# Modulation vectors of a ten-phase transformer kernel: the accumulator folded by DMAs instead of summed by four matmuls

## The reference, cut to what matters

```python
c_act = jax.nn.silu(c)
for layer in range(DEPTH):
    mod = c_act @ ada_w[layer] + ada_b[layer]
    sh1, sc1, g1, sh2, sc2, g2 = [m[:, None, :] for m in jnp.split(mod, 6, axis=-1)]
    hmix = rmsnorm(x, norm_mix[layer]) * (1.0 + sc1) + sh1
    ...
    x = x + g1 * y
```

## Time and profile before

| what | value |
|---|---|
| median of three runs | 1736.61 us (1735.37 to 1739.26) |
| span of the profiled execution | 1734.1 us |
| PE busy | 1708.0 us (98%) |
| DVE busy | 1412.9 us (81%) |
| POOL busy | 435.0 us, of which 267.3 us issue tiles of ada (448 DMAs) |
| DMA | 411.45 MB, mean 237 GB/s |
| PE L2535, the sums in misc | 216 rows, mean 241 ns |
| DVE L2927, multiply-adds of 128 x 512 | 420 rows, mean 751 ns |

### The profile page before, as it was taken

How to read it: one execution, slowest core, us unless ns; L and a number is a source line. 1 busy time by engine, 2 the same in 40 slices (tenths; PEclk the granted TensorE clock), 3 DMA queues, 4 the chain that set the end, 5 groups by cost and what they waited for, 6 DMA issues and landing times. The chain is left out here.

```text
span 1734.1 us, 36503 instructions
## 1 busy us (share of the span) xinstructions
PE 1708.0 (98%) x14039; PEld 1667.7 (96%) x14039; DVE 1412.9 (81%) x1924; ACT 908.4 (52%) x1274; POOL 435.0 (25%) x685
## 2 busy tenths in 40 slices
PE   7999999999999999999999999999999999999998
PEld 5999999999999999999999999999999998799998
DVE  6877898788778977898987799779988896788655
ACT  3443367764335533365634356667444567764444
POOL 6322321012223122321232224540322232401000
PEclk9999999999999999999999999999999999999999
DMA  9998858549887787867698865334988772257550
GB/s 338 356 359 279 294 178 280 166 158 321 304 304 242 276 302 270 302 212 272 229 314 305 302 199 191 115 132 156 322 297 293 230 199 83 78 199 251 184 176 25
DMA packets 261793, 411.45 MB, mean 237 GB/s; under 512 B 21950, under 2 KB 204414, under 8 KB 261560
## 3 DMA queue, kind: packets, MB, share of 16 engines
q1 hardware_dynamic: 224968, 290.67, 51.0%
q0 software_dynamic: 36720, 119.36, 19.4%
HBM read 408.90 MB, written 2.63 MB: 237 GB/s over the span
## 5 line engine op out<-in xcount | busy, mean ns | idle before, releaser
L2891 DVE TENSOR_TENSOR lo<-raw,hi 128x2048 fp32r<-128x2048 f32 (+2 forms) x251 | 565.6, 2256 | 162.4 <-ACT hi L2719 161.8
L2719 ACT CAST hi<-raw 128x2048 fp32r<-128x2048 f32 (+2 forms) x266 | 497.4, 1872 | 377.6 <-PE dacc L2388 189.4
L2386 PE MATMUL up<-operand_hi,hi 128*128 128x256 f32 x1952 | 553.1, 283 | 1.4 <-DVE lo L2891 1.4
L2387 PE MATMUL up<-operand_lo,hi 128*128 128x256 f32 x1952 | 552.3, 283 | 0.0
L2388 PE MATMUL up<-operand_hi,lo 128*128 128x256 f32 x1952 | 552.3, 283 | 0.0
L2163 POOL DMA_DIRECT2D ada<-in_ada_w_dram x448 | 267.3, 613 | 841.8 <-DVE ada_acc L2927 793.5
L2386 PEld LDWEIGHTS up<-operand_hi,hi 128*128 128x128 f32 x1952 | 374.4, 192 | 2.3 <-DVE lo L2891 2.0
L2388 PEld LDWEIGHTS up<-operand_hi,lo 128*128 128x128 f32 x1952 | 374.5, 192 | 0.0
L2387 PEld LDWEIGHTS up<-operand_lo,hi 128*128 128x128 f32 x1952 | 374.5, 192 | 0.0
L2927 DVE SCALAR_TENSOR_TENSOR ada_acc<-ada,c_col,ada_acc 128x512 f32<-128x512 f32 x420 | 315.3, 751 | 13.8 <-DMA ada<-in_ada_w_dram 0.6
L2386 PE MATMUL dacc<-act_hi,hi 128*128 128x256 f32 x976 | 276.2, 283 | 0.7 <-DVE act_lo L3103 0.7
(11 more groups left out here) (483 smaller groups left out, 2858.2 us busy)
## 6 DMA issues: line engine op xcount, KB each, us to landing
ada<-in_ada_w_dram POOLq DMA_DIRECT2D x448, 256.0 KB, 4.8
raw<-in_ffn_wg_dram SPq DMA_DIRECT2D x88, 512.0 KB, 5.4
raw<-in_ffn_wu_dram SPq DMA_DIRECT2D x88, 512.0 KB, 5.2
raw<-in_ffn_wd_dram SPq DMA_DIRECT2D x88, 512.0 KB, 5.6
raw<-in_ffn_w_up_dram SPq DMA_DIRECT2D x88, 512.0 KB, 4.6
raw<-in_ffn_w_down_dram SPq DMA_DIRECT2D x46, 512.0 KB, 4.6
raw<-in_hg_w_in_dram SPq DMA_DIRECT2D x32, 512.0 KB, 4.8
raw<-in_attn_w_qkv_dram SPq DMA_DIRECT2D x24, 512.0 KB, 7.7
```

The lines of the kernel that those rows point to most:

```text
L2386: pe.matmul(o, stat[0], mov[0], start=start, stop=False, skip_group_check=True)
L2387: pe.matmul(o, stat[0], mov[1], start=False, stop=False, skip_group_check=True)
L2719: last = act.copy(put(slab(hi, s, SPL)), take(slab(raw, s, RAW)))
L2891: last = dve.tensor_tensor(put(slab(lo, s, SPL)), take(slab(raw, s, RAW)), put(slab(hi, s, SPL)).bitcast(F32), ALU.subtract)
```

## The change

Only vectors 2 to 29 are changed.

- A tile is loaded by one DMA, 128 rows on 128 partitions with all 1024 columns, and multiplied and added by one DVE instruction of 128 x 1024.
- When a vector's eight tiles are in `ada_acc` (now 128 x 1024), POOL folds it with three accumulating DMAs, each behind the landing of the one before: partitions 64 to 127 onto 0 to 63, 32 to 63 onto 0 to 31, 16 to 31 onto 0 to 15. A fourth DMA writes the 16 rows to DRAM in pieces of 128 columns, and a fifth reads them back as `folded`, 128 x 128, in which partition 16 a + r holds piece a of row r. The five count on the semaphore `folds`.
- PE sums with one matmul: `folded` against `block_ones`, 128 x 8.
- The first tile of the next vector waits on DVE for all five DMAs of the vector before (`folds`), in place of `ada_summed`.
- In the loop of a five-vector phase POOL's instructions are written out: loads 0 to 3 of the next vector, the fold of this one, loads 4 to 7. PE's sum moves from behind the ups of i = 3 to behind those of i = 4, `mod_vector` with it.
- The last vector of such a phase, and that of G, is folded by POOL in the next phase, around `pre_add`, and summed in the middle of that phase: in feed-forward phases behind the ups of block 2, in the mixers at a place of their own. In A the first tile of vector 7 also waits for the fold of vector 6.
- At the start two more small DMAs bring `c` in another layout, and the transpose of `c` has 48 rows instead of 32.

The diff, cut to its core:

```diff
@@ ada_load @@
             source = ada_source(v, k) if source is None else source
+            if v >= 2:
+                eng.dma_start(ada_place(m), source).then_inc(full, 16)
+                return
...
@@ start, SP @@
                 sp.dma_start(c_rows[r0:r0 + ASTEPS, 0:AQ],
-                             T[name].rearrange("b (i q) -> (b i) q", q=AQ)).then_inc(S["c_in"], 16)
+                             T[name].rearrange("b (i q) -> (b i) q", q=AQ)).then_inc(S["lam_in"], 16)
+                sp.dma_start(c_wide[2 * ASTEPS + r0 // AG:2 * ASTEPS + r0 // AG + KB, :],
+                             T[name].rearrange("b (k p) -> (b k) p", p=P)).then_inc(S["lam_in"], 16)
...
@@ POOL @@
+            def fold_start(v):
+                pool.wait_ge(S["ada_step"], tile_steps(tile_index(v, KB - 1) + 1))
+                if v > 2:
+                    pool.wait_ge(S["folds"], 16 * FOLDS * (v - 2))
+                pool.dma_start(ada_acc[0:64, :], ada_acc[64:128, :], accum_op=ALU.add).then_inc(S["folds"], 16)
+            def fold_rest(v):
+                n = v - 2
+                done = 16 * FOLDS * n
+                pool.wait_ge(S["folds"], done + 16)
+                pool.dma_start(ada_acc[0:32, :], ada_acc[32:64, :], accum_op=ALU.add).then_inc(S["folds"], 16)
+                pool.wait_ge(S["folds"], done + 32)
+                pool.dma_start(ada_acc[0:16, :], ada_acc[16:32, :], accum_op=ALU.add).then_inc(S["folds"], 16)
+                pool.wait_ge(S["folds"], done + 48)
+                pool.dma_start(fold_dram.rearrange("(a r) j -> r a j", a=KB),
+                               ada_acc[0:16, :].rearrange("r (a j) -> r a j", a=KB)).then_inc(S["folds"], 16)
+                pool.wait_ge(S["folds"], done + 64)
+                pool.wait_ge(S["ada_summed"], v)
+                pool.dma_start(folded[:, :], fold_dram).then_inc(S["folds"], 16)
...
+                    if left_vector(p) is not None:
+                        fold_start(left_vector(p))
                     pre_add(p)
+                    if left_vector(p) is not None:
+                        fold_rest(left_vector(p))
...
-                        with pool.Fori(0, (FI - 3) // 2) as it:
+                        for u in range(v, v + 4):
                             for k in range(KB):
-                                ada_load(pool, v + 1, k, it, w[u // n][k * P:(k + 1) * P, bass.ds(it * D + (u % n) * D, D)])
+                                if k == ATILES:
+                                    fold_start(u)
+                                    fold_rest(u)
+                                ada_load(pool, u + 1, k)
@@ ada_sum, PE @@
-                pe.wait_ge(S["ada_step"], tile_steps(tile_index(v, KB - 1) + 1) + ASTEPS * it)
                 if v >= 2:
+                    pe.wait_ge(S["folds"], 16 * FOLDS * (v - 1) + 16 * FOLDS * it)
                     pe.wait_ge(S["mod_done"], v + it)
+                    pe.matmul(o[:, 0:KB], folded[:, :], block_ones[:, :], start=True, stop=True,
+                              skip_group_check=True).then_inc(S["ada_summed"], 1)
+                    return
...
@@ ffn, PE @@
                 ups(2)
+                if left_vector(p) is not None:
+                    ada_sum(left_vector(p))
                 down(1)
...
-                        if p in five_vectors and i == 3:
+                        if p in five_vectors and i == 4:
                             ada_sum(v, it)
...
-                if p in five_vectors:
-                    ada_sum(v + 4)
@@ ada_tile, DVE @@
+                if v >= 2:
+                    c = c_col[:, 2 * ASTEPS + (KB if v >= V2 else 0) + k:2 * ASTEPS + (KB if v >= V2 else 0) + k + 1]
+                    if k == 0:
+                        dve.wait_ge(S["ada_summed"], 2)
+                        dve.wait_ge(S["folds"], 16 * FOLDS * (v - 2) + 16 * FOLDS * it)
+                        dve.tensor_scalar(ada_acc[:, :], ada_place(m), c, None, ALU.mult).then_inc(S["ada_step"], 1)
+                        return
+                    dve.wait_ge(S["ada_step"], tile_steps(m) + KB * it)
+                    dve.scalar_tensor_tensor(ada_acc[:, :], ada_place(m), c, ada_acc[:, :],
+                                             ALU.mult, ALU.add).then_inc(S["ada_step"], 1)
+                    return
```

More of the change, by code:

```diff
@@ L52 @@
 ASTEPS = KB * AG
+C_ROWS = 2 * ASTEPS + 2 * KB
+FOLDS = 5
 PE_TILES = KB // 2
@@ L124, in build @@
         ada_acc = sb("ada_acc", D)
+        folded = sb("folded", P)
         operand_hi = sb("operand_hi", KB * SEQ, F32R)
@@ L611, in pe_attention @@
             columns(2)
-            columns(3, lambda: square_sums(0))
+            columns(3, lambda: (square_sums(0), ada_sum(left_vector("A"), o=bank(up, 1))))
             key_spread(0)
@@ L1002, in pe_gating @@
                 col_product(b + 6 + m, bank(up, m))
+            pe.wait_ge(S["gelu_done"], 4)
+            ada_sum(left_vector("G"), o=bank(dacc, 0))
             pe.wait_ge(S["ws_done"], 1)
@@ L1123, in dve_gating @@
             split_lo_half(b + 8, 1)
+            mod_vector(left_vector("G"), psum=bank(dacc, 0))
             gate(0)
@@ L1817, in pe_nsa @@
             compressed_scores()
+            ada_sum(left_vector("N"), o=bank(dacc, 3)[:, SEQ:SEQ + KB])
             pe.wait_ge(S["w1_in"], 64)
@@ L2028, in dve_nsa @@
             split_lo(b + 8)
+            mod_vector(left_vector("N"), psum=bank(dacc, 3)[:, SEQ:SEQ + KB])
             query_rest(3)
@@ L2659, in _ @@
             pe.wait_ge(S["const_done"], 1)
-            pe.transpose(bank(misc, 0)[:, 0:2 * ASTEPS], c_wide[0:2 * ASTEPS, :],
-                         ident[0:2 * ASTEPS, 0:2 * ASTEPS]).then_inc(S["start_pe"], 1)
+            pe.transpose(bank(misc, 0)[:, 0:C_ROWS], c_wide[0:C_ROWS, :], ident[0:C_ROWS, 0:C_ROWS]).then_inc(S["start_pe"], 1)
             pe.wait_ge(S["x_loaded"], 16)
@@ L2865, in _ @@
             act.wait_ge(S["start_pe"], 1)
-            act.activation(c_col[:, :], bank(misc, 0)[:, 0:2 * ASTEPS], ACT.Silu).then_inc(S["start_act"], 1)
+            act.activation(c_col[:, :], bank(misc, 0)[:, 0:C_ROWS], ACT.Silu).then_inc(S["start_act"], 1)
             for c in range(4):
@@ L2914, in ada_tile @@
                 full, count = tile_full(m)
-                dve.wait_ge(full, count + 32 * AG * it)
-                if k == 0 and v > 1:
-                    dve.wait_ge(S["ada_summed"], v + it)
+                dve.wait_ge(full, count + 32 * it)
+                if v >= 2:
[9 more added lines that the diff above has]
+                    return
                 acc = acc_of(v)
@@ L2977, in norm @@
                                              ALU.add, ALU.subtract).then_inc(S["norm_lo"], 1)
-                if left_vector(name) is not None:
-                    mod_vector(left_vector(name))
                 if n == 0:
@@ L3143, in ffn @@
                 iteration(1, 0, v, 0, (0, 2, 2), ahead=p in raw_first)
-                iteration(2, 0, v, 4, (2, 1, 1))
+                iteration(2, 0, v, 4, (2, 1, 1), summed=left_vector(p))
                 if p in gained:
@@ L3148, in ffn @@
                     more = p in five_vectors
-                    iteration(3, it, v + 1 if more else None, 0, (0, 0, 4), summed=v if more else None)
+                    iteration(3, it, v + 1 if more else None, 0, (0, 0, 4))
                     if p in gained:
                         gain_update(p, 0, it)
-                    iteration(4, it, v + 1 if more else None, 4, (2, 0, 2) if conv else (1, 1, 2))
+                    iteration(4, it, v + 1 if more else None, 4, (2, 0, 2) if conv else (1, 1, 2), summed=v if more else None)
                     if p in gained:
@@ L3163, in _ @@
             link(dve.tensor_reduce(group_ones[:, :], ident.rearrange("p (q g) -> p g q", g=AG), AX, ALU.add))
+            link(dve.tensor_reduce(block_ones[:, :], ident.rearrange("p (a r) -> p a r", a=KB), AX, ALU.add))
             dve.wait_ge(S["start_act"], 1)
```

39 lines of the change are left out of this document (23 added, 16 removed).

## The result

| | before | after |
|---|---|---|
| median of the runs, same session | 1737.3 us (1735.4 to 1739.3) | 1881.3 us (1877.4 to 1884.5) |
| ratio | | 1.083 (95% interval 1.081 to 1.084) |
| span of the profiled execution | 1734.1 us | 1877.3 us |
| TensorE's mean granted clock | 1.00 | 0.96 |

The change makes the kernel 8.3% slower, and the time is far outside the range of 1722 to 1806. Direction and mechanism came as forecast; the fold is longer than I had it.

A forecast was written before the change was run, and what follows sets the result against it. PE, busy for 98% of the span, was taken to bound the kernel. Savings and small costs of -11.7 us and fold losses of +36.1 (14.0 + 12.8 + 9.3) net +24.4 on 1736.6: 1761 us, range 1722 to 1806.

The forecast's parts named there:

- the threshold: Fold time t above which DVE's chain outlasts PE's pass: 16.8 us in the F phases, 14.9 in C0.
- DVE's own part: DVE's work in a loop pass without the fold: 18.0 us in F1, 19.9 in C0.
- t, the length of the fold: Time from a vector's last multiply-add to the fifth fold DMA's landing: 18.4 us, bounds 16.7 and 28.7.
- 4t - 70.1: PE's loss in each of F0 to F3 by a late DVE: 3.5 us at t = 18.4, 14.0 together.
- 4t - 60.8: PE's loss in C0, where DVE also does the taps: 12.8 us at t = 18.4.
- 9.3: Loss in us from DVE entering the residual late: 2.0 in each F phase, 1.3 in C0.
- -11.7: Sum in us of cheaper PE sums, sums moved inside phases, G's shorter wait and two start DMAs: -13.2 + 1.7 - 1.1 + 0.9.
- The bounds: Limits for the fold's t: 16.7 us at least; 28.7 at most, with each step priced as a small DMA at the crowded start.
- the fold is hidden: Rival: with t of 16 us or less PE isn't held in the F phases, time 1726 us; chance 0.27.
- 1736.6 - 13.2 + 1.7 - 1.1 + 0.9 - 4.0: Time before; 22 cheaper sums; six sums now inside phases; G's shorter wait; two start DMAs; earlier residuals in five phases.
- Dearer DMAs: Rival: accumulating DMAs, or small ones under load, cost more; t = 21 gives 1813 us; chance 0.13 for above 1803.
- The matmul doesn't get cheap: Rival: most of a PE sum is its start, so the 13.2 us saved shrinks towards 5, 1769 instead of 1761.

The follow-up runs named there:

- experiment 8: Changed kernel, but the next vector's first tile waits for four fold DMAs instead of five, not for the read back from DRAM: 1835.9 us.
- experiment 1: Changed kernel with three plain copies in place of the three accumulating DMAs, same sizes, order and waits: 1876.2 us.
- 3, fold 1 ahead of load 3: Changed kernel with each loop vector's first fold DMA issued before load 3 of the next vector instead of behind it: 1871.0 us.
- 7, two loads held back: Changed kernel with the whole fold issued ahead of loads 2 and 3 of the next vector in the loops, instead of ahead of load 4: 1847.5 us.
- 11, fold ahead of all loads: Changed kernel, one buffer, with the whole fold ahead of all eight loads of the next vector on POOL in the loops: 1872.4 us.
- experiment 2: Changed kernel without the three accumulating DMAs and the waits between them, only 16 of 128 partitions summed: 1718.7 us.
- experiment 6: Kernel before with only the wide tiles (one transfer, one multiply-add per tile), no fold, eight matmuls per sum: 1756.5 us, ratio 1.011.

## Why the prediction was wrong

**What bounds the kernel, and the mechanism: right.** PE was full, DVE's chain got the fold, `lo` came late, PE waited for it 20 times, 1.9 to 6.5 us each. The form of the sum held too. Above the threshold each microsecond of DVE's pass is paid 20 times. The kernels whose passes are all above it show this. "t" is the mean time from a vector's last multiply-add to the next vector's first, "W" that from there to its last; both are from DVE's rows, 20 of each. The last column is 1881.3 plus 20 times the change of t + W. As t + W is the length of a pass, it shows where the time is lost; that t is the cause is shown by experiment 8, which shortens t alone and whose time was forecast:

| kernel | t | W | measured | by 20 (t + W) |
|---|---|---|---|---|
| changed kernel | 24.9 | 18.0 | 1881.3 | 1881.3 |
| 1, plain copies | 24.6 | 18.0 | 1876.2 | 1876 |
| 3, fold 1 ahead of load 3 | 24.5 | 18.0 | 1871.0 | 1874 |
| 7, two loads held back | 22.8 | 18.6 | 1847.5 | 1851 |
| 8, four DMAs | 22.5 | 18.0 | 1835.9 | 1834 |
| 11, fold ahead of all loads | 24.0 | 18.6 | 1872.4 | 1875 |

**DVE's own part: right.** 18.0 us were forecast for a pass and 19.9 for C0; in the loops it takes 17.5 in F0 and F1 and 19.7 in C0.

**The step that failed: t, the length of the fold.** I had 18.4 us and called everything above 20.5 unlikely; it is 24.9. With the 24.8 of the passes behind the first in the prediction's own sum (4t - 70.1 for each of F0 to F3, 4t - 60.8 for C0, the 1.5 us for the first pass taken away again as it didn't show, 9.3 and -11.7) the forecast would have been some 1883, so nothing else of size is missing. By its steps from landing to landing, forecast and mean of the 20 passes: load 3 and fold 1, 5.9 and 9.9; fold 2, 3.4 and 6.0; fold 3, 3.1 and 3.7; the write, 3.0 and 2.9; the read, 3.0 and 2.4. Fold 1 is 4.0 of the 6.5 us and fold 2 another 2.5. (In the F1 pass shown above fold 1 has 9.8 and fold 2 4.9.)

Two readings went wrong there. The first: I priced load 3 and fold 1 from the earlier trace rows, where two DMAs of 256 KB land in 3.8 and 4.3 us. The engines were as full there, but a load was two DMAs of half the size, and the row is near the best of that kernel: of its 20 loads in the same place the later DMA lands in 4.2 to 7.0 us, and the earlier trace rows has 6.1 and 7.0. In the changed kernel load 3 lands 7.8 us after its issue, and fold 1 lands 9.0 us after its own, at 445.24. At the same moment lands the later of two DMAs of weights that SP issued at 433.66 and 434.13, 11.1 us after its issue, the last number of the row below: the DMAs of both queues end together, at a share of 1.05.

```profile
DMA to landing us min/median/max: 6.0/8.6/11.1
```

The second: I took folds 2 and 3 as quiet because the earlier trace rows has a share of 0.34. That window lies 5.6 to 9.6 us behind the end of a vector's last tile. By the trace the 20 such places of the kernel before have 0.64 on average, so the row was a low one, and from 6 to 18.4 us behind the last tile, where I had folds 2 to 5, the average is 0.76. In the changed kernel it is 0.99 there: the weights have 0.80 instead of 0.71, and POOL's queue has 0.19 instead of 0.05, with the end of load 3 and the folds themselves. The bounds stood in the prediction with 28.7 at the upper end (230 us above the kernel before by the same sum, not 250), from the only small DMA under load; I left that end out "as not belonging to this stretch". It did belong, and the range should have reached it at least half-way: t = 25 by the same sum is 1893.

**The rival "the fold is hidden": its price was right, its condition was not met.** 1726 was forecast for it, and experiment 2, which takes the wait away, gives 1718.7. Fully hidden the prediction's own terms give 1736.6 - 13.2 + 1.7 - 1.1 + 0.9 - 4.0 = 1720.9. The Trainium skill ("DMA: Bandwidth & Descriptors", the anatomy of a DMA from GpSimd) has 2.0 us plus bytes over 436 GB/s, by which, as an estimate, fold 1 is 2.6 us and the last two are 2.2. The write and the read agree at 2.3 and 2.1; the quiet fold 1 takes 3.5, and in the loop it takes 9.0. The measurement decides: here the fit holds for the small DMAs with nothing of their queue ahead, and not for fold 1 even at a quiet moment. The same page, in its section on queues, rings and completion order, states for DMAs that SP or ACT issue that a semaphore increment lands only behind all earlier writes of the same DMA engine, across queues. For the DMAs of POOL it doesn't say so there. The weights that land together with fold 1, 11.1 us after their issue, would agree with it, but no run tells this order from mere sharing of bandwidth.

**"Dearer DMAs": the right side, too small** (t = 21, 1813), and not for the first reason in its name: experiment 1 shows that in the loops an addition takes at most 0.4 us more than a copy. The second, small DMAs under load, fits fold 2, which took 2.5 us more than forecast. The largest part is fold 1 behind load 3.

**"The matmul doesn't get cheap": wrong, as weighed.** A sum is two rows and 0.29 us in PE's timeline now, and experiment 2 saves more than the terms for it said. Experiment 6 shows the other sign of the same term.

**What would show it:** the waits for `lo` and for `folded` were found where they were named, and most in C0, as forecast. But they are 18 to 25 us in each five-vector phase, not 5 to 15, and the distance of the folds is 2.1 to 10.1 us, not 2.8 to 3.5.

What stays open: how the 5.7 us that stay without the queue's own loads come about, and whether by bandwidth or by the order of landing. That they are the weights' is argued, not shown: to run the fold without the weights' traffic in a loop wasn't tried. A high share alone doesn't do it, for fold 1 of A's own vector, with no load ahead, took 3.5 us at a share of 0.88.

## What to carry to other kernels

A chain of dependent DMAs on an engine's path is to be priced by what the same queue has in it at that moment and by how full the DMA engines are over many passes, not by one quiet row of the old kernel. Multiply its excess by the passes: here every microsecond above the threshold cost 20. Where such a chain can't be made short, give it a buffer of its own and order the issuing engine by due times: nothing that waits for the next pass ahead of a step of the chain, and no step that waits long ahead of a load that is due; each step left out (here one fold against one more matmul) is worth more than a better price for it.

## What the runs showed of the hardware

- In the loops a DMA that adds 256 KB or 128 KB onto other partitions lands nearly as a plain copy does: on average in 9.0 and 8.8 us for fold 1, 5.7 and 5.3 for fold 2. With little other traffic the addition shows: 3.1 and 2.2 us for the 128 KB of fold 2, at A's start as at N's.
- The adding DMA of 256 KB takes 3.5 us at a quiet moment, 4.7 with only another queue's traffic, and 9.0 behind its own queue's loads as well. Outside the loops of the changed kernel it takes 6.9 to 8.7 us at the four places where loads stand ahead of it and 3.5 to 4.7 at the four where none do.
- A write to DRAM of 64 KB in pieces of 512 bytes and the read back take 2.3 and 2.1 us at the median in the changed kernel, where nothing of their own queue is ahead of them.
- PE's 20 stalls of 1.9 to 6.5 us were all followed by stretches at a granted clock of 0.50. Over the program this made PE's busy time 48 us longer than that of experiment 2 with as many instructions. It took the place of waiting, as DVE and the fold set the length of the passes.
